# A hybrid decoder layer: the step lists of three engines, for the mixer and the cross attention, in another order

## The reference, cut to what matters

```
h = x + [hgrn2(q,f,i,g) || sliding_window_gqa(q,k,v)] @ w_out     where all come from rms_norm(x) @ w_in
h = h + cross_attention(rms_norm(h), rms_norm(mem))               4 heads of 128, 256 rows of memory
h = h + (relu(rms_norm(h) @ mlp_up) ** 2) @ mlp_down              d_ff 4096
```

## Time and profile before

| | us |
|---|---|
| median of 3 runs | 2505.91 |
| lowest, highest | 2505.61, 2506.54 |
| the profiled execution's own time | 2505.29 |
| its span, first to last instruction | 2503.5 |
| mixer, four blocks (77.5 to 819.4) | 741.9 |
| cross part, two turns (819.4 to 1266.2) | 446.8 |
| MLP (1266.2 to 2503.5) | 1237.3 |

### The profile page before, as it was taken

The page is one execution under the profiler, slowest core; times in us unless marked ns, Lnnn a source line. Parts: engine busy times, 40 slices in busy tenths (PEclk is TensorE's granted clock), DMA queues, the critical chain, the costliest instruction groups (busy, mean ns, idle before and its releaser), DMA issues.

```text
span 2503.5 us, 39355 instructions
## 1 busy us (share of the span) xinstructions
PE 2453.5 (98%) x14110; PEld 2011.6 (80%) x14110; DVE 1729.3 (69%) x3014; ACT 1137.4 (45%) x2164; POOL 882.5 (35%) x1018
## 2 busy tenths in 40 slices
PE   7999999999998999999999999999999999999999
PEld 5777888888887788778878888788888888888887
DVE  6798788788678375755668767876664544566765
ACT  5565576566566356546653223422222233322231
POOL 1433100000001552564338657476673222232222
PEclk9999999999999999999999999999999999999999
DMA  4532543643633431652253443242348653444664
GB/s 187 177 129 87 210 136 121 206 135 120 212 122 119 177 121 57 248 176 81 86 183 104 146 169 113 97 132 105 114 152 283 205 155 114 132 134 150 209 194 142
DMA packets 186546, 371.54 MB, mean 148 GB/s; under 512 B 13936, under 2 KB 79984, under 8 KB 183664
## 3 DMA queue, kind: packets, MB, share of 16 engines
...
## 4 chain that ended last, share of the span: by engine, by line
PE 77%; DVE 7%; issue 6%; POOL 5%; DMA 3%; ACT 1%; ACTq 0%; SPq 0%; DVEq 0%; POOLq 0%
PE bank L3245 8%; PE bank L3243 8%; PE bank L3247 8%; PE bank L1542 6%; PE bank L1545 6%; PE bank L1552 6%; PE bank L3223 4%; PE bank L3220 4%; PE bank L3219 4%; PE bank L2157 3%; PE bank L2158 3%; PE bank L2162 3%; POOL m_xlo L2710 3%; POOL wlo L2710 3%; PE bank L1626 2%
## 5 line engine op out<-in xcount | busy, mean ns | idle before, releaser
L447 POOL TENSOR_TENSOR wlo<-raw,whi 128x256 fp32r<-128x256 f32 x372 | 316.3, 883 | 949.4 <-ACT whi L1149 513.5
L1542 PE MATMUL bank<-hi,whi 128*128 128x512 f32 x704 | 286.4, 407 | 2.0 <-ACT fg L1112 2.0
L3245 PE MATMUL bank<-lo,whi 128*128 128x512 f32 x896 | 275.8, 389 | 0.0
L3243 PE MATMUL bank<-hi,whi 128*128 128x512 f32 x896 | 275.8, 389 | 0.0
L3247 PE MATMUL bank<-hi,wlo 128*128 128x512 f32 x896 | 275.8, 389 | 0.0
L1545 PE MATMUL bank<-lo,whi 128*128 128x512 f32 x704 | 275.0, 391 | 0.0
L3034 DVE TENSOR_TENSOR lo<-h,hi 128x1024 fp32r<-128x1024 f32 x80 | 124.4, 1555 | 172.4 <-ACT hi L2798 172.3
L2729 POOL TENSOR_TENSOR wlo<-h,whi 128x256 fp32r<-128x256 f32 x160 | 129.2, 830 | 299.1 <-ACT whi L2790 299.1
L2157 PE MATMUL bank<-hi,whi 128*128 128x512 f32 x504 | 203.1, 403 | 7.9 <-ACT whi L1954 5.2
L2158 PE MATMUL bank<-lo,whi 128*128 128x512 f32 x504 | 196.7, 390 | 0.0
L3247 PEld LDWEIGHTS bank<-hi,wlo 128*128 128x128 f32 x896 | 168.2, 188 | 34.9
(11 more groups left out here) (401 smaller groups left out, 5549.9 us busy)
## 6 DMA issues: line engine op xcount, KB each, us to landing
...
```

The costliest lines, as they stand in the source:

```text
L447: last = pool.tensor_tensor(wlo[:, i, cols], raw[:, i, cols], whi[:, i, cols].bitcast(F32), ALU.subtract)
L1542: pe.matmul(out, w, hi[:, k, :], start=k == 0, stop=False)
L3243: pe.matmul(down_bank(i)[:], wh[:, cols], xh[:, i % 2, :], start=K == 0, stop=False)
L3245: pe.matmul(down_bank(i)[:], wh[:, cols], xl[:, i % 2, :], start=False, stop=False)
```

## The change

Three functions that nothing calls (`spread`, `weave`, `panel_steps`) go. Every list of PE, ACT and DVE for blocks 0 to 3 and for both cross turns gets another order; those for the start, and POOL's, stay. Each list holds the same steps as before, but for ACT's and DVE's last steps of a cross turn: `q3.2` to `q3.4` and `S2.4` go from the end of one turn to the start of the next on ACT, and `q3.7` the other way on DVE. No step is changed in itself, and SP's and POOL's programs are the same. The lists run to some 230 lines of the diff; those that the prediction speaks of, with lines left out:

```diff
-def spread(first, second):
...
 ORDERS = {
     "PE": (
...
-        "m0.0 m0.1 T0 n0 s0.0 s0.1 D0 s0.2 s0.3 m0.2 m1.0 m1.1 m1.2 m2.0 m2.1 m2.2 o0.0 o0.1 o0.2 o0.3 V L0 m3.0 m3.1 "
-        "n1 m3.2 m4.0 m4.1 c0 m4.2 m5.0 c2 m5.1 u0 m5.2 m6.0 m6.1 u1 m6.2 m7.0 u2 m7.1 u3 s1.0 p0 T1 s1.1 s1.2 D1 "
-        "s1.3 n2 m7.2 m8.0 m8.1 m8.2 c4 m9.0 m9.1 m9.2 N0 c6 o1.0 o1.1 o1.2 o1.3 u4 m10.0 u5 m10.1 m10.2 m11.0 L1 "
-        "m11.1 m11.2 s2.0 s2.1 u6 m12.0 m12.1 n3 u7 s2.2 m12.2 m13.0 T2 s2.3 p1 D2 m13.1 m13.2 m14.0 c8 m14.1 m14.2 "
-        "m15.0 o2.0 o2.1 m15.1 o2.2 o2.3 c10 L2 u8 m15.2 m16.0 m16.1 m16.2 u9 u10 s3.0 s3.1 u11 p2 n4 T3 s3.2 s3.3 D3 "
...
+        "m0.0 s0.0 s0.1 n0 T0 m0.1 m0.2 m1.0 m1.1 m1.2 D0 s0.2 s0.3 m2.0 m2.1 o0.0 o0.1 o0.2 o0.3 m2.2 L0 V m3.0 n1 "
+        "m3.1 m3.2 m4.0 m4.1 c0 m4.2 m5.0 c2 u0 m5.1 m5.2 m6.0 u1 m6.1 m6.2 u2 m7.0 u3 s1.0 s1.1 s1.2 T1 p0 s1.3 D1 "
+        "n2 m7.1 m7.2 m8.0 m8.1 m8.2 m9.0 c4 o1.0 o1.1 o1.2 o1.3 c6 m9.1 u4 m9.2 m10.0 N0 u5 m10.1 m10.2 m11.0 L1 "
+        "s2.0 s2.1 u6 m11.1 m11.2 m12.0 m12.1 u7 n3 m12.2 T2 p1 s2.2 s2.3 D2 m13.0 m13.1 m13.2 m14.0 c8 o2.0 o2.1 "
+        "o2.2 o2.3 c10 L2 m14.1 m14.2 u8 m15.0 m15.1 m15.2 m16.0 u9 m16.1 m16.2 u10 s3.0 u11 s3.1 s3.2 T3 p2 D3 s3.3 "
...
-        "o2.1 o2.2 o2.3 c10 L2 m15.0 u8 m15.1 m15.2 m16.0 m16.1 m16.2 s3.0 s3.1 s3.2 u9 n4 u10 s3.3 u11 T3 D3 p2 o3.0 "
-        "c12 c14 o3.1 o3.2 o3.3 u12 u13 L3 M0 M1 M2 u14 u15 p3",
...
+        "o2.2 o2.3 c10 L2 m15.0 m15.1 u8 m15.2 m16.0 m16.1 m16.2 s3.0 s3.1 u9 n4 u10 s3.2 s3.3 u11 T3 p2 D3 c12 o3.0 "
+        "c14 o3.1 o3.2 o3.3 L3 u12 u13 M0 u14 M1 M2 u15 p3",
...
     "ACT": (
...
-        "A1 Q2 c8 c9 c10 w16 u8 t14 L2 c11 t15 t16 l0 l1 l2 X u9 n4 u10 u11 l3 e3 T3 l4 l5 l6 l7 A2 G3 c12 c13 Q3 Y "
-        "u12 c14 L3 c15 u13 u14 u15 A3",
...
+        "t14 w15 w16 Q2 c8 c9 L2 c10 c11 u8 t15 t16 l0 l1 u9 n4 e3 u10 l2 u11 X T3 G3 A2 l3 l4 l5 l6 l7 c12 c13 Q3 "
+        "u12 c14 u13 c15 L3 u14 u15 Y A3",
...
     "DVE": (
...
-        "s0.0 s0.1 r0 s0.2 R0 G0 s0.3 h S0 g1 H0 V E0 r1 R1 f1 c0 c1 b1 x0 c2 c3 x1 j1.0 j1.1 G1 x2 x3 j1.2 j1.3 j1.4 "
-        "H1 e1 s1.0 q0 s1.1 q1 q2 s1.2 S1 s1.3 r2 g2 R2 q3 q4 c4 q5 c5 q6 q7 f2 x4 x5 c6 a0 a1 c7 a2 b2 j2.0 j2.1 "
-        "j2.2 j2.3 j2.4 x6 x7 s2.0 e2 G2 E1 r3 s2.1 H2 s2.2 R3 g3 s2.3 S2 f3 c8 a3 c9 x8 b3 j3.0 j3.1 j3.2 c10 c11 a4 "
-        "a5 j3.3 j3.4 x9 x10 x11 E2 s3.0 e3 G3 l0 l1 s3.1 a6 a7 l2 l3 l4 l5 l6 l7 s3.2 H3 S3 s3.3 g4 r4 R4 f4 c12 c13 "
...
+        "r0 G0 s0.0 s0.1 R0 s0.2 s0.3 S0 h V g1 H0 E0 r1 R1 f1 c0 c1 x0 c2 b1 c3 x1 x2 j1.0 j1.1 j1.2 j1.3 x3 j1.4 G1 "
+        "e1 s1.0 s1.1 H1 s1.2 q0 s1.3 q1 q2 r2 R2 q3 g2 S1 q4 f2 c4 q5 c5 x4 q6 x5 q7 c6 c7 b2 j2.0 j2.1 j2.2 j2.3 "
+        "j2.4 x6 x7 e2 a0 s2.0 G2 E1 a1 H2 r3 s2.1 a2 s2.2 g3 S2 R3 s2.3 f3 c8 a3 b3 c9 x8 j3.0 c10 a4 j3.1 c11 a5 "
+        "j3.2 x9 x10 j3.3 j3.4 x11 E2 e3 l0 s3.0 G3 s3.1 l1 l2 a6 a7 S3 l3 l4 l5 l6 l7 s3.2 s3.3 g4 H3 r4 R4 f4 c12 "
...
 CROSS_ORDERS = {
...
     "ACT": (
...
-        "w1 q3.5- S2.5- q3.6- q3.7- q0.0 S2.6- S2.7- d1.0 w2 N3- w3 d1.1 d1.2 q0.1 S3.0- S3.1- S3.2- w4 w5 q0.2 q0.3 "
-        "S3.3- S3.4- S3.5- S3.6- d1.3 d1.4 d1.5 d1.6 w6 d1.7 w7 w8 w9 q0.4 q0.5 q0.6 w10 q0.7 N0 S3.7- w11 a0.0 w12 "
...
+        "w1 q3.2- q3.3- q3.4- q3.5- S2.4- S2.5- S2.6- S2.7- q3.6- q3.7- d1.0 w2 d1.1 N3- w3 w4 d1.2 d1.3 d1.4 q0.0 w5 "
+        "S3.0- S3.1- S3.2- S3.3- d1.5 S3.4- S3.5- d1.6 q0.1 w6 w7 d1.7 q0.2 q0.3 S3.6- w8 w9 w10 q0.4 q0.5 q0.6 q0.7 "
...
     "DVE": (
...
-        "t0 q3.7- t1 W3.0- d1.0 d1.1 W3.1- W3.2- W3.3- t2 W3.4- W3.5- W3.6- q0.0 q0.1 t3 t4 W3.7- d1.2 d1.3 d1.4 d1.5 "
...
+        "t0 t1 W3.0- W3.1- W3.2- W3.3- t2 t3 d1.0 W3.4- W3.5- d1.1 d1.2 q0.0 W3.6- W3.7- t4 t5 d1.3 d1.4 q0.1 q0.2 "
...
```

More of the change, by code:

```diff
@@ L189, in order @@
         yield (STEP_NAMES[token[0]],) + tuple(int(n) for n in token[1:].split(".") if n)
[L192 to L196, removed]
-        for _ in range(places.count(n)):
-            yield from second[:1]
-            second = second[1:]
-    yield from second
-def panel_steps(panels, products_of):
-    pending = []
-    for i in panels:
-        split = [("split_panel", i + 1)]
-        for n in products_of(i):
-            for part in range(3):
-                yield split + [("make", n, part)] + pending
-                split, pending = [], []
-            pending = [("take", n)]
-    yield pending
 ROW_FIRST, ROW_0, ROW_1, ROW_2, ROW_3 = range(5)
```

## The result

The changed kernel, called after from here on, takes 2513.92 us (median of 8 runs, 2510.51 to 2515.26) where the kernel before took 2506.19 beside it (2504.25 to 2508.50): ratio 1.0028, 95% interval 1.0019 to 1.0038. It is slower; faster, 2499, was forecast. The profiled execution took 2512.69, with a span of 2510.9 (before 2503.5).

| | before | after | difference | forecast |
|---|---|---|---|---|
| block 0 | 197.71 | 199.74 | +2.0 | -3.7 |
| blocks 1 and 2 | 185.17, 185.27 | 185.28, 185.11 | 0 | 0 |
| block 3 | 173.77 | 171.44 | -2.3 | -2.4 |
| first cross turn | 218.69 | 222.50 | +3.8 | 0 |
| second cross turn | 228.14 | 231.65 | +3.5 | 0 |

The account below looks back on a forecast made before the run. TensorE, busy for 98% of the span, was taken as the bound, so only its waits could be won. Terms -1.3 - 2.3 + 1.0 - 1.1 + 0 - 2.4 + 0 - 0.7 = -6.8 gave 2499.1; range 2489 to 2508.

Parts of the forecast that it names:

- Step 1: Start of block 0: the wait of L0 for ACT's squares goes, -1.3.
- Step 2: Block 0 up to s2.0, paced by VectorE: waits of 4.9 fall to 2.6, -2.3 (bounds -4.9 and 0).
- rival B: Block 0 stays at VectorE's pace, slowed by POOL's pieces; five moved instructions cost 3.2 more: about 2502.5, chance 0.25.
- Step 3: Block 0, what step 2 gives back: a0 to a2 now ahead of S2, which c8 needs, +1 (0 to +4.2).
- Step 4: End of block 0: waits at u10, p2 and D3 go, -2.4, against +1.3 at s3.2; together -1.1.
- Step 5: Blocks 1 and 2: VectorE's spare time hides the new order, 0 (bounds 0 and +6 each).
- rival C: Slower: in blocks 1 and 2 the heads' first states come late and PE waits in each; 2511.5, chance 0.10.
- Step 6: Tail of block 3: waits met, -5.1, against +2.65 at c12 behind S3; -2.4 in all (-5.1 to +1).
- Step 8: PE's gaps over all lists: 272 changes from products to small steps and back, not 274; -0.7.
- Step 7: Cross turns: 0, between -2 and +2; panel 7 of the second could come 0 to 1.8 later.
- Rival D: Tail of block 3: waits make the clock fall on M0 to M2, +5.4, so 2504.5; chance 0.05.

Follow-up runs that it names:

- e9_x3: After, with x3 put ahead of j1.2 in VectorE's list of block 0, where it stood behind j1.3: ratio to before 1.0030, block 0 200.76.
- e7_warm: After, with 16 unused 128x512 matmuls on TensorE ahead of m7.0's wait in the second cross turn: ratio to before 1.0016, that turn 229.21.
- e3_w5: After, with w5 put behind store S3.3 in ScalarE's list of the second cross turn: ratio to before 1.0020, that turn 226.60.
- e13_warm4: After, with unused matmuls in four TensorE waits (u3, s3.2, m36.0, m7.0): 2508.09, ratio to before 1.0011.
- e5_turn0: After, with the three lists of the first cross turn in the order of before: ratio to before 1.0014, that turn 219.71.

## Why the prediction was wrong

**Step 1** was right: `L0`'s wait is gone. **Step 2** failed in its mechanism. It took 3.15 of VectorE's idle time as usable ahead of `s2.0` and gave -2.3. Some of that idle time did go (ahead of `x0` 0.42 is left of 1.86), and the waits at `c4` and `u4` went, but 1.24 at `u0`, 3.65 at `u3` and 1.50 at `s2.0` come to 5.3 without three gaps of 0.35, against 4.9 before: nothing gained. I read that `x4` and `a0` to `a2` had moved and not that `x3` now stands behind two more joins. e9_x3 shows that even that was no loss of its own: PE waits there or one step later. What VectorE's pace is there the trace shows: two joins beside POOL's pieces take 4.0 more. This is rival B's outcome and its mechanism, at `j1.1`, `j1.3` and `l4` to `l7` and not at the five instructions that B named, of which one ran beside a piece (1.23). I had spread 19.3 over 88 pieces; what counts is which steps run beside one. How much of the waits goes back to the pieces no run here shows. **Step 3** priced a wait at `c8` at +1; there was none. **Step 4** was -1.1: the waits at `u10`, `p2` and `D3` went as forecast, but `s3.2` took 2.42, where +1.3 was said, `c10` 1.62, and `m17.1` three of 0.83, because `l3` to `l7` had gone behind `S3` and there ran beside pieces. That last one was not seen at all. **Step 5** (blocks 1 and 2, and with it the refusal of rival C) was right: 185.28 and 185.11. **Step 6** was right to 0.1 in its sum, -2.3, and that was luck in part: the one wait stands at `c12`, as forecast, but takes 4.29 and not 2 to 3, and `T3` still waits 0.93; and the step took no gap of 0.35 off its waits. What made up for it are waits that it had not counted: `c14` waited 1.65 in before and 0.31 in after, `u13` 1.78 and 0.92. **Step 8**'s 0.7 can't be told apart.

**Step 7** is where the sign was lost: 0, between -2 and +2, against +7.3. Of the second turn it named the chain, `w5` ahead of the stores, and priced it at `w5`'s work, 1.06; what counts is `w5`'s own wait for its panel, which held `S3.0` until 1065.12. Panel 7 was even a little earlier in the turn (SP's load of `h` 33.0 into it, 33.4 before), but PE came to `m7.0` 2 sooner and waited 4.52, where the same weight load in before waited 3.04; `m7.0` started 43.5 into the turn (44.1 before) and then ran at half clock. So the wait alone made the turn no longer: behind `m7.0`'s start it is 4.1 longer, of which 2.4 are the clock (e7_warm); the other 1.7 are there in e3_w5 and e7_warm too, and were not traced to a step. The first turn was not worked out at all. Its products 30 and 31 stand behind three steps of attention, `N2` comes 3.5 later in the turn (198.8, against 195.3), and VectorE has the `W` steps of the late norm ahead of `t34` to `t36`, for which products wait.

**The clock** made more than half of the loss by the profiles, 4.2 of 7.4, and the prediction had put nothing for it. Rival D had the mechanism, at 0.05 and in the tail, on `M0` to `M2`; in the tail the fall stayed where it was, and it came in three other waits. I asked of each wait how long it was and not what it leaves behind. The Trainium skill's "TensorE: Matmul & The Clock Gate", section "HAM oscillation — how this bites in real kernels", which the prediction cited for the tail, says that a wait between groups of matmuls lets the next group start at half: e7_warm and e13_warm4 agree, with 2.4 for one wait and, by the ratios, 4.3 for four.

So the +7.4 of the profiled span comes from: block 0 +2.0, of which 1.8 is clock (199.74 against 197.98 in e13_warm4); block 3 -2.3; the first turn +3.8, of which 2.8 goes with its lists (e5_turn0; of the chains in it, the ones by `t33` and `t36` are seen in traces, and no kernel removed them all); the second turn +3.5, of which 2.4 is clock (e7_warm) and 1.1, the net of the rest, is open; and +0.4 from what lies around. The clock's part is shown by the two kernels with unused matmuls, and is of single profiles, as the table of block 0 shows.
